# Delta stage of a two-block layer stack: wider products over four PSUM banks, with VectorE and DMA work moved

## The reference

```python
def gated_delta_chunked(q, k, v, g, beta):
    kb = k * beta[..., None]
    A = jnp.einsum('bhnid,bhnjd->bhnij', kb, k) * decay * strict
    T = lax.linalg.triangular_solve(eye + A, eye)
    u = jnp.einsum('bhnij,bhnjd->bhnid', T, v * beta[..., None])
    w = jnp.einsum('bhnij,bhnjd->bhnid', T, kb * jnp.exp(gc)[..., None])
    qk = jnp.einsum('bhnid,bhnjd->bhnij', q, k) * decay
    def step(Sst, inp):
        v_new = u_n - jnp.einsum('bhid,bhde->bhie', w_n, Sst)
        o = jnp.einsum('bhid,bhde->bhie', qd_n, Sst) + jnp.einsum('bhij,bhje->bhie', qk_n, v_new)
        Sst = Sst * jnp.exp(gl_n)[..., None, None] + jnp.einsum('bhid,bhie->bhde', ke_n, v_new)
        return Sst, o
```

## Time and profile before

| | |
|---|---|
| Median of 3 runs (2615.5 to 2616.4) | 2615.65 us |
| The profiled execution's own time | 2616.3 us |
| Its span, first to last instruction | 2614.7 us |
| TensorE busy | 2598.5 us, 99% |
| VectorE busy | 2000.0 us, 76% |
| ScalarE busy | 1317.2 us, 50% |
| TensorE's granted clock, mean | 0.999 |
| The delta stage, chunks of groups 0 to 3 | 1357.3 to 1788.3 us of the span |

### The profile page before, as it was taken

One profiled execution on the slowest core, in us unless ns is written; L12 is line 12 of the kernel. 1 busy time (PEld: TensorE's weight loads), 2 busy tenths in 40 slices (PEclk: granted clock), 3 DMA queues, 4 the chain that ended last, 5 costly groups with the idle time before them and its releaser, 6 DMA issues.

```text
span 2614.7 us, 36953 instructions
## 1 busy us (share of the span) xinstructions
PE 2598.5 (99%) x13412; PEld 2217.7 (85%) x13412; DVE 2000.0 (76%) x2800; ACT 1317.2 (50%) x1663; POOL 163.1 (6%) x332
## 2 busy tenths in 40 slices
PE   9999999999999999999999999999999999999998
PEld 7888888888888888888889999998888888788887
DVE  5887877776756868777467786976798899989565
ACT  5444444444444445444456455454656666564453
POOL 0000000000000000000001241413000000000000
PEclk9999999999999999999999999999999999999999
DMA  8555555555676566566655555655565665666754
GB/s 307 179 188 176 181 185 185 184 188 192 195 192 202 188 200 201 186 204 214 195 195 169 169 166 160 197 158 167 185 197 190 195 195 185 197 192 193 249 174 159
DMA packets 151499, 499.06 MB, mean 191 GB/s; under 512 B 28720, under 2 KB 29456, under 8 KB 150832
## 3 DMA queue, kind: packets, MB, share of 16 engines
q1 hardware_dynamic: 148736, 486.19, 57.3%
q0 software_dynamic: 2608, 10.74, 1.3%
HBM read 492.66 MB, written 4.21 MB: 190 GB/s over the span
## 4 chain that ended last, share of the span: by engine, by line
PE 92%; DVE 3%; POOL 2%; DMA 1%; issue 1%; ACT 1%; SPq 0%; DVEq 0%; ACTq 0%; POOLq 0%
PE PS L1978 24%; PE PS L1979 24%; PE PS L1980 24%; PE PS L2017 5%; PE PS L2003 3%; PE PS L2005 3%; PE PS L2006 3%; PE PS L2022 2%; PE PS L2158 2%; POOL xi L594 1%; POOL xt L590 1%; DVE wlo L1103 1%; DVE yl L1672 1%; PE PS L2030 0%; PE PS L2165 0%
## 5 line engine op out<-in xcount | busy, mean ns | idle before, releaser
L651 ACT CAST whi<-raw 128x1024 fp32r<-128x1024 f32 x899 | 940.3, 1050 | 1177.4 <-PE PS L1980 905.3
L1103 DVE TENSOR_TENSOR wlo<-raw,whi 128x1024 fp32r<-128x1024 f32 x899 | 1097.5, 1225 | 546.4 <-ACT whi L651 541.6
L1978 PE MATMUL PS<-whi,aHL 128*128 128x512 f32 x1904 | 744.3, 391 | 3.4 <-DVE wlo L1162 2.0
L1980 PE MATMUL PS<-whi,aHL 128*128 128x512 f32 x1904 | 741.1, 389 | 0.0
L1979 PE MATMUL PS<-wlo,aHL 128*128 128x512 f32 x1904 | 741.0, 389 | 0.0
L1978 PEld LDWEIGHTS PS<-whi,aHL 128*128 128x128 f32 x1904 | 357.5, 188 | 78.5 <-issue 2.4
L1980 PEld LDWEIGHTS PS<-whi,aHL 128*128 128x128 f32 x1904 | 357.4, 188 | 74.6
L1979 PEld LDWEIGHTS PS<-wlo,aHL 128*128 128x128 f32 x1904 | 357.6, 188 | 72.8
L2003 PE MATMUL PS<-aHL,whi 128*128 128x256 f32 x768 | 220.9, 288 | 1.5 <-DVE aHL L1139 1.5
L2006 PE MATMUL PS<-aHL,wlo 128*128 128x256 f32 x768 | 217.2, 283 | 0.0
L2005 PE MATMUL PS<-aHL,whi 128*128 128x256 f32 x768 | 217.2, 283 | 0.0
(11 more groups left out here) (360 smaller groups left out, 2879.4 us busy)
## 6 DMA issues: line engine op xcount, KB each, us to landing
raw<-in_stream SPq DMA_DIRECT2D x900, 512.0 KB, 3.4
xT<-in_xT SPq DMA_DIRECT2D x4, 512.0 KB, 6.5
H<-in_x SPq DMA_DIRECT2D x4, 512.0 KB, 9.1
pB<-in_pool_b POOLq DMA_DIRECT2D x4, 512.0 KB, 5.5
iT<-diag_in SPq DMA_DIRECT2D x16, 128.0 KB, 3.5
bg<-in_b_gate POOLq DMA_DIRECT2D x8, 256.0 KB, 4.0
out<-eb SPq DMA_DIRECT2D x8, 256.0 KB, 2.1
dmask<-in_dmask SPq DMA_DIRECT2D x4, 384.0 KB, 5.0
```

Source lines behind the costliest of these rows:

```text
L651: nc.scalar.copy(whi[:, s], raw[:, s]).then_inc(hi_done, 1 + blank)
L1103: nc.vector.tensor_tensor(wlo[:, s], raw[:, s], whi[:, s].bitcast(F32), ALU.subtract).then_inc(lo_done, 1 + blank)
L1978: mm(out, hi[:, kt + k, tok], whi[:, s, k], start=kt + k == 0, stop=False)
L1980: ins = mm(out, lo[:, kt + k, tok], whi[:, s, k], start=False, stop=last and k == KPC - 1)
```

## The change

`chunk_d` takes the place of `chunk_b`: a product of 512 columns (`whi` by `aH` and `aL`) and one of 256 (`wlo` by `aH`) for each 128 channels. A projection now fills banks 0 to 3, each with two halves, and k, q and v all use these banks. z stays in banks 2 and 3. The first and the last chunk of a projection are worked through in pieces of two, one and one banks (v's last chunk takes banks 2 and 3 first, where z comes next). At the end of each piece ScalarE copies the high half into `kqv` (`high_halves`), VectorE adds the other half (`halves_added`), and only then TensorE may start that piece of the next projection. For this, VectorE's subtraction of chunk j+4 of j = 6, 14 and 22 is made after the additions. k's sums lie in the place of v (`held`). The taps read `kqv` and not PSUM. z's Silu stands ahead of the last cast of a group.

Moved besides: `ke` from j = 14 to j = 20, `aT` from 13 to 12, q's norms from 21 to 26, the decays from 6 to 4 (their DMA from 2 to 0), the blocks' DMAs from 15, 16, 29 and 30 to 13, 14, 27 and 28, the transpose of `iU` to j = 31 of its own group, the output's scaling from n = 46 to 51, its transposes to j = 0, 2, 3, 5 and 6 of the group after the next, and its split to j = 10 there. A few semaphores are merged.

The diff, cut:

```diff
@@ -84,6 +84,7 @@
 ADD_AT = (9, 17)
 SUM_AT = ((11, 13, 15, 18, 19, 20), (21, 23, 24, 25, 26, 27))
 SPLIT_AT = (22, 29)
+O_TURNS = {0: range(0, 2), 2: range(2, 6), 3: range(6, 8), 5: range(8, 12), 6: range(12, 16)}
 NORM1_AT = {0: 2, 1: 3, 4: 4, 5: 5, 6: 6, 7: 7}
 
 
@@ -374,6 +375,14 @@
         def wide(b):
 
             return PS[:, 4 - 4 * b:8 - 4 * b]
+
+        def held(y):
+
+            return 2 if y == 0 else y
+
+        def pieces(y):
+
+            return (slice(2, 4), slice(0, 1), slice(1, 2)) if y == 2 else (slice(0, 2), slice(2, 3), slice(3, 4))
 
         def steps_before(i, b):
 
@@ -459,7 +468,7 @@
                 q = i * (D_PER // RING) + (D_AT // RING + 2)
                 for j in range(D_PER):
                     chunk(q + j // RING, j % RING)
-                    if not first and j == 2:
+                    if not first and j == 0:
                         sp.wait_ge(qk_sb, i)
                         decays_in(i)
                     if first and j == 11:
                                          aT[cut].rearrange("p t h n -> p (t h) n")[:, :, cut]).then_inc(scratch_out, 16)
-                    if j == 16:
+                    if j == 14:
                         sp.wait_ge(scratch_out, i * 128 + 80)
                         for r in range(P // BLK):
                             sp.dma_start(xn[r * BLK:(r + 1) * BLK],
                                          diag_in.rearrange("b m r c -> (b m) (r c)")).then_inc(xn_in, 16)
-                    if j == LV - 5:
...
                 if n == LV + 6:
+                    if i:
+                        act.wait_ge(t_ps, (T_D + i) * 2)
                     act.wait_ge(rec_ps, i * REC + R1)
...
-                if n == (LV + 24 if i < D_N - 1 else LV + 14):
+                if n == (2 * D_PER + 10 if i < D_N - 1 else LV + 14):
                     t_split_hi(i + T_D, oaH, i * QT, lambda c: C_DN, turned=oD_turned if i < D_N - 1 else None)
 
+            def high_halves(i, q, y):
+
+                if y == 0 and i:
+                    act.wait_ge(v_turned, i)
+                for n, c in enumerate(pieces(y)):
+                    if n < 2:
+                        act.wait_ge(piece_ps, i * 6 + (2 * y + n + 1))
+                    else:
+                        done(act, q, 8 * y + 7)
+                    nc.scalar.copy(kqv[:, held(y), c], PS[:, c, SEQ:]).then_inc(high_sb, 1)
+
             def conv_first(i, y):
 
+                act.wait_ge(sum_sb, i * 9 + (3 * y + 3))
                 for c in range(HG):
                     w = wcv[:, bass.ds(i * (HG * TAPS) + ((1, 0, 2)[y] * 16 * TAPS + c * TAPS + TAPS - 1), 1)]
-                    nc.scalar.activation(yD[:, c], half(2 * (y % 2), c), ACT.Copy, scale=w).then_inc(conv0_sb, 1)
+                    nc.scalar.activation(yD[:, c], kqv[:, held(y), c], ACT.Copy, scale=w).then_inc(conv0_sb, 1)
 
             def delta(i, first):
                 q = i * (D_PER // RING) + D_AT // RING
@@ -888,11 +911,16 @@
                         y = 1 if j == 20 else 2
                         act.wait_ge(conv_tap, i * 36 + 12 * (y + 1))
                         nc.scalar.activation(kqv[:, y], yD[:], ACT.Silu).then_inc(kqv_sb, 1)
+                    if j in (7, 15, 23):
+                        high_halves(i, q, j // 8)
+                    if j == D_PER - 1:
+                        done(act, q, j)
+                        nc.scalar.activation(zD[:], PS[:, 2:4], ACT.Silu).then_inc(zd_sb, 1)
                     split_hi(q, j + RING)
                     if first and j in (2, 4):
                         norm3((j + 2) // 2)
                     if first and j == 4:
-                        act.wait_ge(ba_in, 64)
+                        act.wait_ge(ba_in, 80)
                         for n in (0, 2, 3):
                             ins = nc.scalar.copy(wbp[:, :, n * 32:(n + 1) * 32], wbr[:])
                         ins.then_inc(small_hi, 1)
...
@@ -1507,7 +1532,7 @@
                     dve.wait_ge(esq_sb, i + 1)
                     nc.vector.scalar_tensor_tensor(out=oms[:, 1], in0=oms[:, 0], scalar=1.0 / P, in1=esq[:], op0=ALU.mult,
                                                    op1=ALU.add).then_inc(omean_sb, 1)
-                if n == LV + 12:
+                if n == (LV + 17 if i < D_N - 1 else LV + 12):
...
                     ins.then_inc(od_sb, 1)
-                if i < D_N - 1 and n in (LV + 16, LV + 17, LV + 18, LV + 20):
-                    m = (LV + 16, LV + 17, LV + 18, LV + 20).index(n)
-                    if m == 0:
+                if i < D_N - 1 and n - 2 * D_PER in O_TURNS:
+                    steps = O_TURNS[n - 2 * D_PER]
+                    if steps[0] == 0:
                         dve.wait_ge(od_sb, i + 1)
-                    ins = turn(oD, oD_turned, range(4 * m, 4 * m + 4))
-                    if m == 3:
+                    ins = turn(oD, oD_turned, steps)
+                    if steps[-1] == 15:
                         ins.then_inc(t_ps, 2)
-                if n == (LV + 24 if i < D_N - 1 else LV + 14):
+                if n == (2 * D_PER + 10 if i < D_N - 1 else LV + 14):
                     t_split_lo(i + T_D, oaH, oaL, i * QT, lambda c: C_DN, turned=oD_turned if i < D_N - 1 else None)
                 if n == D_PER + 1:
...
+
+                for n, c in enumerate(pieces(y)):
+                    dve.wait_ge(high_sb, i * 9 + (3 * y + n + 1))
+                    nc.vector.tensor_tensor(kqv[:, held(y), c], PS[:, c, 0:SEQ], kqv[:, held(y), c], ALU.add).then_inc(sum_sb, 1)
 
             def norms(i, n):
                 dve.wait_ge(sq_sb, i * 2 + (n + 1))
@@ -1576,7 +1607,13 @@
                     if first and j == 11:
                         dve.wait_ge(ba_ps, 4)
                         log_decays(i, heads(6))
-                    split_lo(q, j + RING)
+                    if j in (7, 15, 23):
+                        halves_added(i, j // 8)
+                        split_lo(q, j - 1 + RING)
+                    if j == LV - 3:
+                        block_turn(i)
+                    if j not in (6, 14, 22):
+                        split_lo(q, j + RING)
                     if first and j in (2, 4):
                         norm3((j + 2) // 2)
...
-                        done(dve, q, j)
                     if first and j == 14:
                         dve.wait_ge(cum_sb, 4)
                         nc.vector.tensor_scalar(necum[:], ecum[:], -1.0, None, ALU.mult)
                     if j == 12:
                         norms(i, 0)
                         key_scales(i)
-                    if j == 13:
                         dve.wait_ge(dt_sb, i + 1)
                         dve.wait_ge(en_sb, i * 4 + 4)
                         nc.vector.tensor_tensor(ed[:], en[:, 0, 0], dT[:, 0, :, P - 1], ALU.mult).then_inc(ke_sb, 1)
@@ -1623,15 +1657,16 @@
                                                                      scalar=en[:, 1, t, h:h + 1], in1=dT[:, t, h],
                                                                      op0=ALU.mult, op1=ALU.mult)
                         ins.then_inc(a_sb, 1)
-                    if j == 14:
+                    if j == 20:
                         dve.wait_ge(ke_sb, i * 2 + 1)
                         for h in range(HG):
                             ins = nc.vector.tensor_scalar(ke[:, h], heads(6)[:, 0, h], ed[:, h:h + 1], None, ALU.mult)
                         ins.then_inc(ke_sb, 1)
                     if 15 <= j <= 17:
                         conv(i, 1, j - 14)
+                    if j == 26:
+                        norms(i, 1)
                     if j == 21:
-                        norms(i, 1)
                         dve.wait_ge(qk_ps, i + 1)
                         for t in range(NT):
                             for h in range(HG):
...
+                ins.then_inc(multiplied, 1)
+
+            def chunk_d(q, j, kt, order, ready):
+
+
+                s = j % RING
+                pe.wait_ge(lo_done, q * RING + (RING + j + 1))
+                first, last = kt == 0, kt == (K16 - 1) * KPC
+                for n, c in enumerate(order if first or last else [slice(0, QT)]):
+                    if first:
+                        pe.wait_ge(*ready[n])
+                    tiles = range(c.start, c.stop)
+                    for k in range(KPC):
+                        for c in tiles:
+                            mm(PS[:, c], whi[:, s, k, c * P:(c + 1) * P], aHL[:, kt + k].rearrange("p a n -> p (a n)"),
+                               start=kt + k == 0, stop=False, skip_group_check=True)
+                    for k in range(KPC):
+                        for c in tiles:
+                            ins = mm(PS[:, c, 0:SEQ], wlo[:, s, k, c * P:(c + 1) * P], aH[:, kt + k], start=False,
+                                     stop=last and k == KPC - 1, skip_group_check=True)
+                    if last and n < 2:
+                        ins.then_inc(piece_ps, 1)
                 ins.then_inc(multiplied, 1)
...
```

(19 more changed lines are left out.)

73 lines of the change are left out of this document (30 added, 43 removed).

## The result

The changed kernel takes **2622.31 us**, median of twelve runs (2620.6 to 2623.9), beside 2616.25 us of the kernel before on the same chip: a ratio of 1.0022, with a 95% interval from 1.0013 to 1.0031. The prediction said 2613.8 us and no change, within 2607.5 to 2618.7. It was slower, by 6 us, and outside the range.

A forecast was written before the change was run, and what follows sets the result against it. TensorE, busy 99% of the span, was taken as the bound. Terms -8.6 + 2.4 + 4.7 + 0.3 - 0.6 = -1.8 us gave 2613.8 us, called no change, with a range of 2607.5 to 2618.7.

The forecast's parts named there:

- The products: Delta stage: 96 chunks go from 2.88 to 2.79 us with wide products, 8.6 us less.
- rival 3: Wide products no quicker here than two narrow ones: gain 2 us, time 2620.4; chance 0.05, half of it slower.
- The handovers: TensorE waits for copied and added sums at j = 8, 16, 24: eight handovers of 0.3 us, 2.4 us more.
- `ke`: TensorE waits at j = 21: 0.85 us in group 0, 1.3 in three others; 4.7 more, bounds 0 and 2 a group.
- At nothing: Work priced at zero: added copies and additions, output's transposes and split in the gated stage, taps, decays, norms, merged semaphores.
- `iT`: The inverse's path comes 3 to 7 us earlier, so TensorE's wait for this transpose goes: 0.6 us less.
- z's Silu: Next group's second piece waits for it: ready after 1.32 us, first piece takes 1.40, so no cost.
- the added copies and additions: Nine each a group, some 4.5 us on each engine, lie in ScalarE's and VectorE's idle time: no cost.
- the first chunk: Start of the delta stage: its second piece waits for the copy `eE`, 0.3 us more.
- The lead of a late subtraction: Chunk 23's subtraction ends 6.1 us before TensorE starts that chunk, so late subtractions are covered.
- The rivals: Three alternatives: `ke` costs nothing (2609.1 or 2606.7; 0.24), handovers run late (2623; 0.07), wide products no quicker (2620.4; 0.05).
- Rival 2: ScalarE or VectorE busy when a handover's first piece ends: 10 us more over eight handovers, 2623; chance 0.07.

The follow-up runs named there:

- e12: Changed kernel with `ke` at j = 14, copies ahead of the output's transposes, a four-piece handover, and 512-column products cut into two of 256: 2616.46 us.
- e6: Changed kernel with `ke` at j = 14, copies ahead of the output's transposes, and the handover in four one-bank pieces: 2608.56 us, ratio 0.9977.
- e1: Changed kernel with `ke` computed at j = 14 again, all else kept: 2612.83 us, ratio 0.9991.
- e7: Changed kernel leaving out all but the first step of GpSimd's inverse of the 32x32 blocks: 2618.24 us.
- e9: Changed kernel with ScalarE's Silu of q at j = 20 put behind that chunk's cast: one run, 2619.23 us.
- e2: Changed kernel with the late chain's step ahead of the output's transposes in VectorE's list of the gated stage: 2620.64 us.
- e4: Changed kernel with each 512-column product cut into two of 256 into the same bank: 2627.53 us.
- e5: Changed kernel with `ke` at j = 14 again and the gated stage's late-chain copies ahead of the output's transposes: 2611.03 us, ratio 0.9982.
- e10: Changed kernel with `ke` and the output's scaling both at j = 14 again: 2615.64 us, ratio 0.9997.

## Why the prediction was wrong

- **The products** (-8.6 us): right in kind, 0.7 too large. e12 gives 7.9. The 0.09 us a chunk holds for chunks that follow one another; of those behind another product of the late chain the trace shows 0.07 to 0.08. So rival 3, with 2 us, falls. The Trainium skill, TensorE: Matmul & The Clock Gate, section Back-to-back issue gap, gives the rule of rival 3 for a single product and not for a stream of them with weight loads, and the trace does not agree with it: 0.12 and 0.23 us from start to start.
- **The handovers** (+2.4): right. e6 takes them away and gains 2.5, by the medians and by the chunks. Within them two parts were off, and that they nearly cancelled was luck: ScalarE started earlier by 0.06 us, TensorE 0.10 later.
- **`ke`** (+4.7): **the step that failed.** The wait, its place and the four groups were right, but the term of 4.7 us was too small: it measured 9.6 us (chunk 21 of the changed kernel less that of e1). Of the 4.9 too little, by the runs: 2.0 is the scaling beside GpSimd (e7: chunk 21 is 0.75, 0.58 and 0.74 us shorter in groups 1 to 3, the last against 7.54), 0.6 the table load of group 0 (e9), 1.65 the clock behind the wait (group 3, 9.19 us for 7.54), 0.4 the step from VectorE to TensorE, four times 0.1; 0.2 is left over. The forecast took the scaling's 2.10 us from the earlier trace rows, at a place where GpSimd stood still, and moved it under GpSimd's work; the earlier trace rows had shown when GpSimd starts. And it listed ScalarE's part as one cast, where its list had the Silu ahead of it.
- **At nothing**, the output's transposes in the gated stage: **the second step that failed**, +1.5. VectorE is busy there for 76 of 110 us, but a share says nothing about the order: two copies for which TensorE waits stood behind the transposes in the list (e2).
- **The clock** was no term at all. A wait was priced at its length. In the profiles after the change and of the experiments, 12 waits for `ke` of 1.8 to 2.0 us were followed three times by a fallen clock (in the changed kernel, e2 and e4, in a different group each time; in e9 never), the seven of over 3 us six times, and the twelve of 0.8 to 1.4 us never. Each fall cost 1.5 to 2.9 us on top. Where the four groups have no wait for `ke` (the kernel before, e1, e5, e6, e10 and e12), no clock falls in them after the stage's first chunk.
- `iT`, z's Silu, the added copies and additions, the first chunk: as forecast. (The lead of a late subtraction, 6.1 us, was counted without the heads' work in chunk 21, 5.46 us and not 2.88; with it and chunk 22's 2.95 it is 8.7. There was more cover than was said.)
- **The rivals.** None decided. Rival 2 is real (e10) but not in this kernel, since `ke` and the scaling had been moved. The slower side was forecast by other mechanisms than the one that brought it, and `ke`'s upper bound of 2 us a group would have been right for the wait alone (2.0), but left the clock out.

So the wide products and the handover are worth 5 to 7.5 us, and where `ke` and the output's transposes stood turned that into a loss of 6.

## What to carry to other kernels

A duration holds for the place where it was measured: before a step is moved on an engine, look at what the other engines do there, and take the whole list ahead of it, on each engine of the chain, table loads too. Work moved into a stretch with idle time can still stand in front of the one instruction that TensorE waits for; put the awaited one first in the loop's body, which cost nothing here (e2). If a result can be made seven chunks ahead of its reader, leave it there, and let the first piece of a handover be the smallest.
